# Moving TensorE's loop over extra expert blocks behind one matmul group, and the 64-token tile to the head of the last stage

## The chip, the cores and the metric

The kernel runs on one core of one Trainium2 chip. The metric is the device time of one execution in microseconds (us). Three runs of the kernel before gave 830.54, 830.91 and 832.59 us; the median is 830.91.

## What is computed

The reference is one step of a hybrid decoder layer over 512 prompt tokens and 64 sample tokens, 576 in all, with a model width of 1024. All of it is float32. Only its end matters here:

```python
    moe = jnp.zeros_like(h)
    for e in range(N_EXPERTS):
        gu = jnp.einsum('bld,df->blf', u, w_gate_up[e])
        hid = jax.nn.silu(gu[..., :D_EXPERT]) * gu[..., D_EXPERT:]
        moe = moe + combine[..., e:e + 1] * jnp.einsum('blf,fd->bld', hid, w_down[e])
    h = h + moe
    u = rmsnorm(h, norm_ple)
    gate = jax.nn.sigmoid(jnp.einsum('bld,de->ble', u, w_ple_gate))
    h = h + gate * jnp.einsum('blp,pd->bld', p_l, w_ple_proj)
    ...
    y = rmsnorm(h, norm_final)
```

Each token uses two of sixteen experts. The "input product" is `p_l @ w_ple_proj`, with 256 input channels; the "gate product" is `u @ w_ple_gate`, with 1024.

## The kernel before, in words

The 576 tokens are five tiles: tiles 0 to 3 of 128 tokens and tile 4 of 64. Every engine has one program in order, and semaphores tie the programs together.

**The expert stage.** Tokens are sorted into slots. Twelve phases of 128 slots (`NPH`) run through TensorE, which computes gate and up (L1348), transposes (L1361) and multiplies by the down weights (L1296). The results go to `y_slots` in HBM. Tokens that don't fit go into extra blocks of 32 slots. Extra block 0 is always computed, between the last phases (L1307, L1316, L1324, L1331). Further blocks are a loop that runs `n_ov - 1` times: TensorE reads `n_ov` from memory into a register (L1367), tests it (L1368) and loops (L1369). ScalarE, VectorE, GpSimd and SyncE have the same test in their own programs. In the trace the body of the loop runs on no engine: there is one extra block.

**The input products.** `p_product(t)` (L1376 to L1387) multiplies tile t's input by `w_proj`: 8 matmuls of 512 columns for a tile of 128 tokens, 16 of 256 for tile 4, whose columns go to two halves of the array (`sides`). Tile 0's product is made much earlier. `p_product(1)` waits until all results of the expert stage are out of PSUM (`y_ready` at 24), `p_product(3)` until ScalarE has copied out tile 1's. ScalarE copies each product to memory (`p_evac`, L1440 in the trace, since a helper records it) and counts `pp`. Behind tile 3's copy it loads the table for square roots (L1746).

**The last stage** goes over the tiles in the order `LAST`; k is the place in that order. Its steps for one k:

- GpSimd gathers two rows of `y_slots` per token (L2717, two indirect DMAs, j = 0 and 1) into one of two buffers. For k of 2 and more it first waits for `h3` to reach k: that is, combine(k - 2) has freed the buffer.
- VectorE's combine(k) (L2438) adds both to the residual `h2`, and counts `h3`: twice for k = 0 (by column halves), once for each later k.
- TensorE's `u3_transpose(k)` (L1401) makes eight transposes; VectorE's `u3_evac(k)` (L2449) copies them out in two halves with the gain, and counts `u3T`.
- ScalarE sums squares (L1751) and takes a root (L1754), for all five tiles before anything later; VectorE takes the reciprocal (`r3`, L2455).
- TensorE's gate product (L1419) runs in two column halves, hf 0 and hf 1. Between them stands `u3_transpose(k + 1)`. For k of 1 and more it begins when both halves of `u3_evac(k)` are done; for k = 0 the first half is enough to begin. For k of 2 and more each half waits for ScalarE's sigmoid of k - 2 as well.
- ScalarE takes the sigmoid (L1765) and squares (L1771) by halves, and a root (L1775); VectorE multiplies and adds (`gated`, L2462 and L2463), and `finish(k)` (L2481, L2486) scales the output row; SyncE stores it (L763, L765, L767) and loads the final gain (L758) when `h3` reaches 2.

VectorE's order is written out by hand, with k for the tile in that place:

```python
combine(0); u3_evac(0); combine(1); r3(0); combine(2); r3(1)
combine(3); u3_evac(1); r3(2); combine(4); r3(3); r3(4)
for k in range(NT):
    if 1 <= k < NT - 1: u3_evac(k + 1)
    for hf in range(2): gated(k, hf)      # and mean0 behind the first
    finish(k)
```

So `u3_evac(1)` stands behind combine(2) and combine(3), and `u3_evac(2)` behind all of `gated(0, ...)` and `finish(0)`. `LAST` is [0, 1, 4, 2, 3]: tile 4 is third.

Of the kernel before, what the change touches and what calls it, by code (L numbers as in the profile page):

```python
# [30 lines left out]
NT = 5  # L31
# [8 lines left out]
NOV = 32  # L40
# [4 lines left out]
RING = 3  # L45
GAMMA = [1.0 - 2.0 ** (-5.0 - h) for h in range(H)]
LEVELS = [2, 4, 8, 16, 32, 64]
LAST = [0, 1, 4, 2, 3]
HEADK = [(0, 1), (1, 2), (2, 4), (4, 6), (6, 8)]
ORDER = [4, 1, 0, 3, 2]  # L50
POS = {t: i for i, t in enumerate(ORDER)}
# [5 lines left out]
def ntok(t):  # L57
    return P if t < 4 else NB * LS


def sides(t):

    return [(slice(0, P), slice(0, 512))] if t < 4 else [(slice(0, 64), slice(0, 256)), (slice(64, P), slice(256, 512))]
# [283 lines left out]
def build(nc, a, o):  # L347
# [9 lines left out]
    with ExitStack() as ctx:  # L357
        def sb(name, shape, dt=F32):
            return ctx.enter_context(nc.sbuf_tensor(name, shape, dt))
# [3 lines left out]
        def sem(name):  # L363
            if name not in sems:
                sems[name] = ctx.enter_context(nc.semaphore(name))
            return sems[name]
# [4 lines left out]
        def C(name, n=P):  # L371
            off, w = CAT[name]
            return const[0:n, off:off + w]
# [177 lines left out]
        ovi = sb("ovi", [P, NOV + 1], U32)  # L551
# [124 lines left out]
        def _(sp):  # L676
# [82 lines left out]

            for k, t in enumerate(LAST):  # L760
                sp.wait_ge(sem("y_out"), k + 1)
# [11 lines left out]
        def _(pe):  # L773
# [24 lines left out]
            for s in STEPS:  # L798
# [52 lines left out]
                elif k0 == "tmv":  # L851
                    t = s[1]
# [6 lines left out]
                elif k0 in ("rTq", "rTk"):  # L859
                    t, n = s[1], ntok(s[1])  # L860
# [7 lines left out]
                elif k0 == "rS":  # L868
                    t, n = s[1], ntok(s[1])
# [9 lines left out]
                elif k0 == "rO":  # L879
                    t, n = s[1], ntok(s[1])  # L880
# [42 lines left out]
                elif k0 == "rU":  # L923
                    t = s[1]
# [60 lines left out]
                elif k0 == "gG":  # L985
                    t, n = s[1], ntok(s[1])
# [14 lines left out]
                elif k0 == "gs":  # L1001
                    t, n = s[1], ntok(s[1])
# [5 lines left out]
                elif k0 in ("gK", "gQ"):  # L1008
                    t, n = s[1], ntok(s[1])
# [7 lines left out]
                elif k0 == "gA":  # L1017
                    t, n = s[1], ntok(s[1])
# [5 lines left out]
                elif k0 == "lY":  # L1024
                    _, v, t = s
# [16 lines left out]
                elif k0 in ("lX", "lT"):  # L1042
                    _, v, t = s
# [19 lines left out]
                elif k0 in ("gV", "gk"):  # L1063
                    t, n = s[1], ntok(s[1])
# [7 lines left out]
                elif k0 == "gW":  # L1072
                    t, n = s[1], ntok(s[1])
# [8 lines left out]
                elif k0 == "gU":  # L1082
                    t, n = s[1], ntok(s[1])
# [5 lines left out]
                elif k0 in ("sD", "sDs"):  # L1089
                    t = s[1] if k0 == "sD" else 4  # L1090
# [19 lines left out]
                elif k0 == "sO":  # L1110
                    t, n = s[1], ntok(s[1])
# [30 lines left out]
                elif k0 == "sU":  # L1142
                    t = s[1]
# [15 lines left out]
                elif k0 in ("wo", "wh", "wg"):  # L1159
                    t = s[1]  # L1160
# [42 lines left out]
                elif k0 in ("x2a", "x2b", "x2c"):  # L1203
                    t, n = s[1], ntok(s[1])
# [6 lines left out]
                elif k0 == "rt":  # L1211
                    t, n = s[1], ntok(s[1])
# [8 lines left out]
                elif k0 == "rtT":  # L1221
                    t, n = s[1], ntok(s[1])
                    ev_wait(pe, ("rt", t))
                    nc.tensor.matmul(single[plan.buf[s]][0:n, 0:20], rtp[POS[t] % 2][:, 0:n], C("pick32"), start=True, stop=True).then_inc(s_mm, 1)
                elif k0 == "rank":
                    t, n = s[1], ntok(s[1])
                    i = POS[t]
# [9 lines left out]
                elif k0 == "ids":  # L1237
                    t, n = s[1], ntok(s[1])
                    i = POS[t]
# [62 lines left out]
            def ov_xpose(i):  # L1302

                pe.wait_ge(sem("ov_xg"), 16 * i + 16)
                pe.sem_inc(sem("ov_turn"), 1)
                for k in range(KD):
                    last = nc.tensor.transpose(single[0][:, BS * k:BS * k + BS], xg_ov[:, k * P:(k + 1) * P], C("ident")[0:BS, 0:BS])  # L1307
                last.then_inc(sem("ov_pe"), 1)

            def ov_gu(i):  # L1310

                pe.wait_ge(sem("ov_dve"), 3 * i + 1)
                pe.wait_ge(sem("ov_w"), 32 * i + 32)
                for k in range(KD):
                    for g in range(4):
                        last = nc.tensor.matmul(single[1][BS * g:BS * g + BS, 0:P], xT_ov[:, k, :], w_gu[0][:, k, P * g:P * g + P],  # L1316
                                                start=(k == 0), stop=(k == KD - 1))
                last.then_inc(sem("ov_pe"), 1)

            def ov_hT(i):  # L1320

                pe.wait_ge(sem("ov_dve"), 3 * i + 2)
                pe.sem_inc(sem("ov_turn"), 1)
                nc.tensor.transpose(single[0][:, DE:DE + 64], hid_ov, C("ident")[0:64, 0:64]).then_inc(sem("ov_pe"), 1)  # L1324

            def ov_down(i):

                pe.wait_ge(sem("ov_dve"), 3 * i + 3)
                for k in range(2):
                    for g in range(4):  # L1330
                        last = nc.tensor.matmul(single[1][BS * g:BS * g + BS, DE:2 * DE], hT_ov[:, BS * k:BS * k + BS],  # L1331
                                                w_dn_ov[:, k, DE * g:DE * g + DE], start=(k == 0), stop=(k == 1))
                last.then_inc(sem("ov_pe"), 1)
# [30 lines left out]
            down(NPH - 1)  # L1364
            ov_down(0)

            n_ov = pe.value_load(ovi[0:1, NOV:NOV + 1], min_val=0, max_val=NOV)  # L1367
            with pe.If(n_ov > 1):  # L1368
                with pe.Fori(1, n_ov) as i:  # L1369
                    ov_xpose(i)  # L1370
                    ov_gu(i)
                    ov_hT(i)
                    ov_down(i)

            def p_product(t):

                n = ntok(t)
                if t == 1:
                    pe.wait_ge(sem("y_ready"), 2 * NPH)
                elif t > 2:  # L1380
                    pe.wait_ge(sem("pp"), t - 1)
                for hf in range(2):
                    for k in range(2):
                        for rows, cols in sides(t):
                            last = nc.tensor.matmul(pair[t % 2][rows, hf, cols], pT[:, k, t * P:t * P + n],  # L1385
                                                    w_proj[:, k, hf * 512 + cols.start:hf * 512 + cols.stop], start=(k == 0), stop=(k == 1))
                last.then_inc(sem("pp_mm"), 1)  # L1387

            for t in range(1, NT - 1):
                p_product(t)  # L1390

            def u3_transpose(k):
                t, n = LAST[k], ntok(LAST[k])
                pe.wait_ge(sem("h3"), k + 2 if k else 1)
                if k >= 2:
                    pe.wait_ge(sem("u3T"), 2 * k - 2)
                for c in range(KD):
                    if k == 0 and c == 4:
                        pe.wait_ge(sem("h3"), 2)
                    out = single[2 * (k % 2) + c // 4][:, (c % 4) * n:(c % 4 + 1) * n]  # L1400
                    last = nc.tensor.transpose(out, h2[0:n, t, c * P:(c + 1) * P], C("ident")[0:n, 0:n])  # L1401
                last.then_inc(sem("u3_mm"), 1)

            p_product(NT - 1)
            u3_transpose(0)
            for k, t in enumerate(LAST):
                n = ntok(t)
# [19 lines left out]
        def _(act):  # L1427
# [13 lines left out]
            for s in STEPS:  # L1441
                k0 = s[0]
                if k0 == "ss":
                    for k in range(KD):
                        act.wait_ge(sem(f"ld_x{[k < hi for _, hi in HEADK].index(True)}"), 16)
                        nc.scalar.activation(xsq[:, k, :], uT[:, k, :], ACT.Square).then_inc(sem("xsq"), 1)
# [156 lines left out]
                elif k0 == "gA":  # L1603
# [7 lines left out]
                    last.then_inc(ev(k0), 1)  # L1611
                elif k0 == "lY":
                    _, v, t = s
                    n = ntok(t)
                    mm_wait(act, s)
# [120 lines left out]
            def p_evac(t):  # L1736

                act.wait_ge(sem("pp_mm"), t)
                for rows, cols in sides(t):
                    last = copy(pp[t][0:ntok(t)].rearrange("p (a b) -> p a b", a=2)[:, :, cols], pair[t % 2][rows, :, cols])  # L1740
                last.then_inc(sem("pp"), 1)
# [5 lines left out]
            p_evac(NT - 1)  # L1747
            for k, t in enumerate(LAST):
                n = ntok(t)
# [5 lines left out]
                                     scale=1.0 / D).then_inc(sem("ms_root"), 1)  # L1755
            for k, t in enumerate(LAST):
                n = ntok(t)
# [24 lines left out]
        def _(dve):  # L1782
# [650 lines left out]
            def combine(k):  # L2433
                t, n = LAST[k], ntok(LAST[k])
                for j in range(2):
                    dve.wait_ge(sem(f"ga{j}{k % 2}"), 16 * (k // 2 + 1))
                    for cols in ([slice(0, 512), slice(512, D)] if j and k == 0 else [slice(0, D)]):
                        ins = V.scalar_tensor_tensor(out=h2[0:n, t, cols], in0=ga[k % 2][j][0:n, cols], scalar=wcomb[0:n, j, POS[t]:POS[t] + 1],  # L2438
                                                     in1=h2[0:n, t, cols], op0=ALU.mult, op1=ALU.add)
                        if j == 0:  # L2440
                            link(ins)
                        else:
                            ins.then_inc(sem("h3"), 1)
# [346 lines left out]
```

## Time and profile before

| what | value |
|---|---|
| runs | 830.54, 830.91, 832.59 us |
| profiled execution, its own time | 833.75 us |
| its span | 831.9 us |
| mean granted clock of TensorE | 0.996 of full speed |
| PE (matmul) busy | 811.9 us, 98% |
| VectorE, ScalarE, GpSimd busy | 385.5, 213.8, 150.4 us |
| last matmul of the expert stage ends | 739.6 us after the span's start |
| last matmul of the kernel ends | 824.8 us |

The times in the profile count from the span's start. The chain that ended last is read back from the last instruction: each line of it is a start, a length, and an engine with its output and source line; "issue" is time in which the engine waited for nothing that the profile shows. Register loads, branches and DMA-issuing instructions are not counted as busy. A timeline merges like instructions; in brackets stands the idle time before them and what ended it.

### The profile page before, as it was taken

How to read it: one execution, taken by the hardware profiler on the slowest of the kernel's cores; microseconds unless marked ns; L12 is line 12 of the kernel's file. 1: busy time of each engine (PE TensorE's matmuls, PEld its weight loads, DVE VectorE, ACT ScalarE, POOL GpSimd, SP SyncE). 2: the span in 40 equal slices, each digit the busy share in tenths (PEclk: the TensorE clock that was granted, in tenths of full speed). 3: DMA queues.
4: the chain of work that ended last, by engine and by line, in shares of the span. 5: the costliest groups of instructions: out<-in, count | busy, mean ns of one | idle time of the engine just before them, and what ended most of it. 6: DMA issues, size and time to landing. Idle time of an engine off the chain costs nothing.

```text
span 831.9 us, 12853 instructions
## 1 busy us (share of the span) xinstructions
PE 811.9 (98%) x5194; PEld 509.7 (61%) x5194; DVE 385.5 (46%) x861; ACT 213.8 (26%) x462; POOL 150.4 (18%) x182
## 2 busy tenths in 40 slices
PE   9999999999999999999999999999999999989996
PEld 4545777887889987777777776455343333334452
DVE  3223457584666523664852559636441111005543
ACT  3211152339324311131001101022121111124554
POOL 0234321004055224200220053000100001004000
PEclk9999999999999999999999999999999999999999
DMA  9420354403020200522252024036899999976111
GB/s 363 201 101 10 119 184 152 141 32 110 1 102 3 92 12 13 202 89 84 101 202 100 2 102 180 21 110 253 328 355 406 424 423 410 416 292 222 51 39 51
DMA packets 20896, 135.23 MB, mean 163 GB/s; under 512 B 2420, under 2 KB 3060, under 8 KB 13668
## 3 DMA queue, kind: packets, MB, share of 16 engines
q1 hardware_dynamic: 13392, 103.34, 31.8%
q0 software_dynamic: 4720, 23.83, 7.8%
q10 hardware_dynamic: 2724, 7.21, 2.6%
q8 instruction: 43, 0.70, 0.3%
q14 instruction: 17, 0.14, 0.0%
HBM read 118.94 MB, written 19.63 MB: 167 GB/s over the span
## 4 chain that ended last, share of the span: by engine, by line
PE 46%; DVE 2%; issue 1%; ACT 1%; DVEq 0%; ACTq 0%
PE single L1348 10%; PE pair L1419 8%; PE pair L1200 6%; PE single L961 6%; PE pair L1296 5%; PE pair L982 2%; PE pair L1385 2%; PE single L982 2%; PE single L1281 1%; PE single L1256 1%; PE single L1361 1%; PE single L1401 1%; PE single L1209 0%; PE pair L1252 0%; DVE mem L2179 0%
## 5 line engine op out<-in xcount | busy, mean ns | idle before, releaser
L791 PE MATMUL pair<-mem 128*128 128x288 f32 x640 | 158.9, 408 | 0.0
L791 PEld LDWEIGHTS pair<-mem 128*128 128x128 f32 x640 | 120.3, 190 | 35.6 <-ACT mem L1440 2.1
L961 PE MATMUL single<-mem 128*128 128x288 f32 x448 | 110.0, 407 | 0.2
L961 PEld LDWEIGHTS single<-mem 128*128 128x128 f32 x448 | 84.7, 190 | 25.7 <-issue 1.6
L1348 PE MATMUL single<-mem 128*32 128x512 f32 x768 | 85.1, 594 | 0.9 <-DVE mem L2388 0.9
L1440 ACT ACTIVATE mem<-single 128x256 f32<-128x256 f32 (+5 forms) x109 | 44.6, 419 | 127.0 <-PE single L1209 48.5
L1440 ACT ACTIVATE mem<-pair 128x512 f32<-128x512 f32 (+5 forms) x77 | 33.0, 479 | 165.9 <-PE pair L791 63.1
L1419 PE MATMUL pair<-mem 128*128 128x512 f32 (+1 forms) x192 | 63.3, 524 | 0.8 <-DVE mem L2449 0.8
L1348 PEld LDWEIGHTS single<-mem 128*32 128x32 f32 x768 | 23.6, 110 | 52.8 <-issue 51.7
L2381 DVE SCALAR_TENSOR_TENSOR mem<-single,mem 128x256 f32<-128x256 f32 x12 | 5.8, 484 | 102.3 <-PE single L1348 91.1
L1200 PE MATMUL pair<-mem 128*128 128x512 f32 x112 | 51.0, 601 | 0.0
L1419 PEld LDWEIGHTS pair<-mem 128*128 128x128 f32 (+1 forms) x192 | 28.3, 172 | 32.6 <-issue 29.1
L1296 PE MATMUL pair<-mem 128*32 128x512 f32 x384 | 43.9, 595 | 0.0
L2100 DVE TENSOR_TENSOR mem<-mem,single 128x288 f32<-128x288 f32 x40 | 18.1, 452 | 55.7 <-PE single L961 52.2
L1200 PEld LDWEIGHTS pair<-mem 128*128 128x128 f32 x112 | 20.3, 190 | 21.7 <-issue 21.4
L856 PE MATMUL pair<-mem 128*128 128x512 f32 (+1 forms) x96 | 32.1, 525 | 0.0
L2687 POOL DMA_INDIRECT mem<-u_rows,ids x12 | 11.4, 948 | 110.6 <-PE single L1281 101.0
L832 PE MATMUL pair<-mem 128*128 128x512 f32 x64 | 28.2, 595 | 0.5 <-DVE mem L1812 0.5
L982 PE MATMUL pair<-mem 128*128 128x288 f32 x112 | 28.4, 409 | 0.2
L1898 DVE SCALAR_TENSOR_TENSOR mem<-mem,vec 128x512 f32<-128x512 f32 x36 | 27.9, 774 | 1.3
L982 PE MATMUL single<-mem 128*128 128x288 f32 x112 | 27.8, 406 | 0.0
L982 PEld LDWEIGHTS pair<-mem 128*128 128x128 f32 x112 | 21.0, 190 | 6.9 <-DVE mem L2152 1.3
(413 smaller groups left out, 1087.5 us busy)
## 6 DMA issues: line engine op xcount, KB each, us to landing
mem<-in_w_gu SPq DMA_DIRECT2D x17, 2048.0 KB, 14.7
mem<-in_w_down SPq DMA_DIRECT2D x17, 1024.0 KB, 13.8
y_slots<-mem SPq DMA_DIRECT2D x9, 512.0 KB, 11.0
y_slots<-in_zeros POOLq DMA_DIRECT2D x8, 512.0 KB, 8.0
mem<-in_w_ga SPq DMA_DIRECT2D x2, 2048.0 KB, 8.4
mem<-in_w_gb SPq DMA_DIRECT2D x2, 2048.0 KB, 7.8
mem<-in_w_wo SPq DMA_DIRECT2D x2, 2048.0 KB, 7.6
mem<-in_w_pg SPq DMA_DIRECT2D x2, 2048.0 KB, 17.3
```

Of the source, the lines that this page charges most:

```text
L791: last = nc.tensor.matmul(pb[:, hf, 0:HALF], w(k), rhs[:, k, hf * HALF:(hf + 1) * HALF], start=(k == 0), stop=(k == kk - 1))
L832: last = nc.tensor.matmul(q_bank[t][rows, cols], uT[:, k, t * P:t * P + ntok(t)], ring[0][:, 512 * k + cols.start:512 * k + cols.stop], st ...
L856: last = nc.tensor.matmul(pair[plan.buf[s]][rows, 0, cols], uT[:, k, t * P:t * P + ntok(t)], w[:, k, cols], start=(k == 0), stop=(k == KD ...
L961: last = nc.tensor.matmul(single[plan.buf[s]][:, 0:HALF], lhs[:, k, :], rhs[:, k, :], start=(k == 0 and j in (0, 1, 3, 4)), stop=(k == 3), ...
L982: last = nc.tensor.matmul(fast_bank(s), lhs[:, k, :], rhs[:, k, :], start=(k == 0 and j in (0, 1, 3, 4)), stop=(k == 1), skip_group_check= ...
L1200: last = nc.tensor.matmul(sx_bank[j], rows[:, u, v, :], wgt[:, u, 512 * v:512 * v + 512], start=(i == 0 and j < 5), stop=(i == 3), skip_gr ...
L1296: last = nc.tensor.matmul(pair[p % 2][BS * g:BS * g + BS, n, :], hT[p % 2][:, k, BS * g:BS * g + BS], w_dn[e % 4][:, k, n * 512:(n + 1) * ...
L1348: last = nc.tensor.matmul(single[3][BS * g:BS * g + BS, :], xT[p % 2][:, k, BS * g:BS * g + BS], w_gu[e % 4][:, k, :], start=(k == 0), sto ...
L1419: last = nc.tensor.matmul(pair[(k + 1) % 2][rows, hf, cols], u3T[:, c, t * P:t * P + n], w_pg[hf][:, c, cols], start=(c == 0), stop=(c == ...
L1440: copy = lambda out, in_, scale=1.0: nc.scalar.activation(out, in_, ACT.Copy, scale=scale)
L1898: V.scalar_tensor_tensor(out=acc[m % 2][:, 0:LP], in0=cbuf[m % 2][:, j:j + LP], scalar=conv_w[:, m, j:j + 1], in1=acc[m % 2][:, 0:LP], op0 ...
L2100: V.tensor_tensor(to, plus, single[plan.buf[s]][:, 0:HALF], ALU.add).then_inc(ev(k0), 1)
```

## The change

Two edits. TensorE's register load, test and loop move from before the input products to behind that of tile 1, so that its order is p_product(1), test, p_product(2), p_product(3), p_product(4). And `LAST` begins with the 64-token tile, on every engine that goes by it. The loops of the other engines stay where they are.

```diff
-LAST = [0, 1, 4, 2, 3]
+LAST = [4, 0, 1, 2, 3]
...
             ov_down(0)
 
-            n_ov = pe.value_load(ovi[0:1, NOV:NOV + 1], min_val=0, max_val=NOV)
-            with pe.If(n_ov > 1):
-                with pe.Fori(1, n_ov) as i:
-                    ov_xpose(i)
-                    ov_gu(i)
-                    ov_hT(i)
-                    ov_down(i)
-
             def p_product(t):
...
-            for t in range(1, NT - 1):
+            p_product(1)
+            n_ov = pe.value_load(ovi[0:1, NOV:NOV + 1], min_val=0, max_val=NOV)
+            with pe.If(n_ov > 1):
+                with pe.Fori(1, n_ov) as i:
+                    ov_xpose(i)
+                    ov_gu(i)
+                    ov_hT(i)
+                    ov_down(i)
+
+            for t in range(2, NT - 1):
                 p_product(t)
```

## Rows read from the trace of the kernel before

**Rows 1.** The page, part 1: busy time, share of span, instructions per engine.

```profile
PE 811.9 (98%) x5194; PEld 509.7 (61%) x5194; DVE 385.5 (46%) x861; ACT 213.8 (26%) x462; POOL 150.4 (18%) x182
```

**Rows 2.** The chain that ended last, 738 to 757: start, us, engine, line, count.

```profile
738.76 0.86 PE single L1331 x16
739.62 2.97 issue
742.59 14.14 PE pair L1385 x40
756.74 1.04 PE single L1401 x8
```

**Rows 3.** The same chain over the gate products.

```profile
766.55 13.74 PE pair L1419 x32
...
780.93 10.67 PE pair L1419 x48
...
803.28 0.87 PE single L1401 x8
804.16 20.62 PE pair L1419 x48
```

**Rows 4.** Busy time by stretch: length, engines' busy time, granted clock, DMA share.

```profile
742.60:756.74 14.14, 14.14 (x41) 6.20 (x42) 2.70 (x3) 3.87 (x4) 5.48 (x6) 0.88 0.56 189
```

**Rows 5.** The chain around a semaphore instruction of TensorE's own (L1305).

```profile
721.55 7.00 PE single L1348 x64
728.55 0.61 PE single L1307 x8
```

**Rows 6.** Timeline of VectorE: start, us, line, operation, count, idle before.

```profile
738.83 0.69 DVE L2425 COPY mem<-pair 128x512 f32<-128x512 f32 x1 [1.66 <-PE pair L1296]
750.77 1.28 DVE L2438 SCALAR_TENSOR_TENSOR mem<-mem,wcomb 128x1024 f32<-128x1024 f32 x1 [11.25 <-DMA mem<-y_slots,posu]
753.03 1.41 DVE L2438 SCALAR_TENSOR_TENSOR mem<-mem,wcomb 128x512 f32<-128x512 f32 x2 [0.98 <-DMA mem<-y_slots,posu]
...
759.00 2.59 DVE L2438 SCALAR_TENSOR_TENSOR mem<-mem,wcomb 128x1024 f32<-128x1024 f32 x2
```

**Rows 7.** Timeline of GpSimd: the gathers of the last stage.

```profile
746.54 0.95 POOL L2717 DMA_INDIRECT mem<-y_slots,posu  x1 [49.61 <-DMA y_slots<-mem]
747.79 0.94 POOL L2717 DMA_INDIRECT mem<-y_slots,posu  x1 [0.30 <-issue]
...
754.72 0.91 POOL L2717 DMA_INDIRECT mem<-y_slots,posu  x1 [3.50 <-DVE mem L2438]
...
761.87 1.80 POOL L2717 DMA_INDIRECT mem<-y_slots,posu  x1 [5.04 <-DVE mem L2438]
763.97 1.00 POOL L2717 DMA_INDIRECT mem<-y_slots,posu  x1 [0.30 <-issue]
```

**Rows 8.** Timeline of VectorE, from combine(3) to the second and third copies.

```profile
766.92 1.28 DVE L2438 SCALAR_TENSOR_TENSOR mem<-mem,wcomb 128x1024 f32<-128x1024 f32 x1 [2.69 <-DMA mem<-y_slots,posu]
769.18 1.28 DVE L2438 SCALAR_TENSOR_TENSOR mem<-mem,wcomb 128x1024 f32<-128x1024 f32 x1 [0.97 <-DMA mem<-y_slots,posu]
770.38 1.28 DVE L2449 TENSOR_TENSOR mem<-single,vec 128x512 f32<-128x512 f32 x2
...
771.65 2.58 DVE L2438 SCALAR_TENSOR_TENSOR mem<-mem,wcomb 128x1024 f32<-128x1024 f32 x2
...
785.83 0.75 DVE L2449 TENSOR_TENSOR mem<-single,vec 128x256 f32<-128x256 f32 x2
```

**Rows 9.** Timelines of ScalarE and VectorE: first sigmoids, and tile 4's round.

```profile
777.05 0.69 ACT L1765 ACTIVATE mem<-pair,ms 128x512 f32<-128x512 f32 x1
...
794.36 0.95 ACT L1765 ACTIVATE mem<-pair,ms 64x256 f32<-64x256 f32 x2
...
795.68 0.67 DVE L2462 TENSOR_TENSOR mem<-mem 64x512 f32<-64x512 f32 x1
...
804.20 1.29 DVE L2449 TENSOR_TENSOR mem<-single,vec 128x512 f32<-128x512 f32 x2
```

## The prediction

> **What bounds the kernel now.** I read the page's busy times first. TensorE's matmuls fill 98% of the span [rows 1], so time is saved only where TensorE idles or runs slowly, and lost wherever it is made to wait. The chain that ended last shows the first place. Behind the last matmul of the expert stage (738.76 + 0.86 = 739.62) stand 2.97 us of "issue", in which TensorE waits for nothing the profile shows [rows 2]. That is the register load and the test of the loop over extra blocks. Then come the four input products in 14.14 us. At full rate a matmul of 512 columns takes 13.74 / 32 = 0.43 us, and tile 4's 32 column-split ones take 10.67 - 16 x 0.43 = 3.8 us [rows 3]. So the four should take 3 x 8 x 0.43 + 1.9 = 12.2 us. The granted clock of that stretch was 0.88, a mixture of the levels 2.4 and 1.2 GHz [rows 4]: the idle gap cost 2.97 us, and the lower level behind it some 1.95.
>
> The timelines of GpSimd and VectorE show the second place. The last stage is fed by a relay of gathers. The first issues at 746.54, when the last stores of the expert stage have landed [rows 7], and the combined rows stand at 753.03 + 1.41 = 754.44 [rows 6]. TensorE is done with the input products only at 756.74, so at that moment it is TensorE that is late, by 2.3 us. A little later the relay is close behind: the copy `u3_evac(1)` ends at 771.66 [rows 8], and TensorE needs it when tile 0's gate product is half through the second 13.74, at 766.55 + 6.87 = 773.4 [rows 3]. `u3_evac(2)` ends at 786.6 [rows 8] and is needed at 780.93 + 6.87 = 787.8 [rows 3]. These two slacks, 1.8 and 1.2 us, are what the change plays with.
>
> **Part one, the test behind tile 1's product.** Nothing is added or removed; 16 instructions of TensorE (8 weight loads, 8 matmuls) move ahead of the load and the test. The product waits for the copies out of PSUM, which end at 739.52 [rows 6], so it starts at 739.6, at full clock, and ends at 743.05. The test runs beside it if TensorE's sequencer goes on while matmuls are queued. For that speaks a semaphore increment that TensorE's program has ahead of L1307: the matmuls on both sides of it join without a gap (721.55 + 7.00 = 728.55) [rows 5]. A register load from memory isn't such an increment, so both ends stay: wholly hidden, tile 2's product starts at 743.05; not hidden, at 746.0, with the lower clock again. I take 743.9: the 16 instructions issued in under 1 us, then the same gap, of which 0.9 us shows. Tiles 2, 3 and 4 then end at 743.9 + 2 x 3.43 + 1.9 = 752.7, which is 4.0 us earlier than now.
>
> The Trainium skill, "TensorE: Matmul & The Clock Gate", section "Part 2: What happens when you issue a matmul", says that the sequencer pops the next instruction as soon as it has committed one to the engine, and the table at its head gives TensorE's queue 64 places. By it the stage ends 4.0 us earlier; without it, at 756.7 as now. Against it stands "Runtime: NRT & Kernel Launch", section "Instruction fetch mechanics": a taken branch to a page that isn't loaded must wait for its fetch. No row here tells how much of the 2.97 us is such a fetch; as the fetch too would run beside queued matmuls, it would change the sum only if it came to more than the gap seen.
>
> Behind the waiting sequencer are tiles 2 to 4; ScalarE waits for tile 1's product, and gets it earlier.
>
> **Part two, tile 4 first.** No matmul is added. Tile 4's gate product takes 2 x 3.8 = 7.6 us where tile 0's takes 13.7, so TensorE asks for everything behind it 6 us sooner. The relay can't follow. VectorE's operations go by columns and cost the same for 64 rows as for 128. I follow the relay step by step.
>
> k = 0. Its gathers issue at 746.54 and 747.79 as now [rows 7]. They move half the bytes; the second lands at 753.03 now, and I take 752.3 (751.5 to 753.0: no row shows a landing of 64 rows by itself). combine(0) ends 1.41 later, 753.7; TensorE's transposes at 754.05, the copy (0.75 for 64 tokens, [rows 8]) at 754.8. TensorE starts the product behind the first half of the copy, 754.4, and without a wait would be through at 754.4 + 3.8 + 1.0 + 3.8 = 763.0, the 1.0 for the next tile's transposes [rows 2].
>
> k = 1. The gathers follow at once; the second issues at 750.3 and lands 5.24 later (747.79 to 753.03), at 755.5. combine(1) is two operations of 1.28 behind the copy: 757.2, against 759.00 + 2.59 = 761.6 now [rows 6]. So of the 4 us that TensorE gains, the relay takes 4.4 here.
>
> k = 2. Issued when combine(0) ends plus 0.28 [rows 6, 7]: 754.0 and 755.2. At 5.2 us each the second lands at 760.4; combine(2) ends at 761.7.
>
> k = 3. Issued 0.35 behind combine(1), 757.55; the second 1.25 to 2.1 later (between 761.87 and 763.97 it was 2.1, as the first took 1.80) [rows 7]. It lands 5.21 behind its issue (763.97 to 769.18): 764.4. combine(3) ends at 765.7, and `u3_evac(1)`, 1.28 long, at 767.0. Only then may TensorE begin k = 1: it **idles from 763.0 to 767.0**. That is the wait that takes the place of the one removed.
>
> k = 4. Issued behind combine(2), 762.0 and 763.25; landed at 768.5; combine(4) ends at 769.8. From there ScalarE's first sigmoid follows after 777.05 - (771.65 + 2.58) = 2.8 us: 772.6. Tile 4's round of sigmoid, `gated` and `finish` takes 804.20 - 794.36 = 9.84 us, less 0.37 in which VectorE was still busy with a copy (795.68 - 795.31) [rows 9]; for a tile of 128 it is 8.8. So `u3_evac(2)` ends at 772.6 + 9.5 + 1.29 = 783.4. TensorE would ask for it at 767.0 + 6.87 + 0.95 + 6.87 = 781.7, and at 783.65 if the 4.0 us of idle time bring the lower clock as the 2.97 did, at the same 1.95. I take the later, 783.7.
>
> From there all is TensorE's: 6.87 + 0.95 + 13.74 + 0.95 + 20.62 = 43.1 us (0.95 for eight transposes, between the 1.04 and 0.87 of [rows 2, 3]), end at 826.8. Now it ends at 804.16 + 20.62 = 824.8. The tail is the same, tile 3 being last in both. **Sum: +2.0 us**, against the profiled execution's own 833.75 us (span 831.9) 835.75. That execution is 2.84 above the median of the runs, and its last stage shows no reason for that; I put the 2.0 on the median: 832.9 us. The stores keep their places on SyncE's queue: every `y_out` comes in VectorE's order as before.
>
> The bounds of this case: with every gather landing 4.23 us behind its issue, as the first one does (746.54 to 750.77), `u3_evac(1)` ends at 764.2 and `u3_evac(2)` at 780.7, which is -1.0 us. With 1 us more in each of the three generations of gathers, as three loads at once could cost, it is +5.0.
>
> **Rivals.**
> - The test isn't hidden. Then `u3_transpose(0)` stays at 756.7, combine(1) ends at 760.8, `u3_evac(1)` at 771.1, combine(4) at 773.8, `u3_evac(2)` at 787.4, and the end comes at 830.5: +5.7 us, 836.6, slower. Its point: it decides once the input products end later than 753. For it: nothing in the trace shows TensorE's register load beside matmuls. Against it: the increment [rows 5].
> - The clock. TensorE idles 4 us before k = 1, longer than the 2.97 that brought the lower level. If that lasts twice as long as behind the first gap, TensorE asks at 785.6, +3.9 us, 834.8.
> - TensorE alone sets the time: the relay keeps up, and the 4.0 us of part one arrive whole, 826.9. For that `u3_evac(1)` must end by 763.0 and `u3_evac(2)` by 777.7, so combine(4) by 764.1, about when I expect the gather before it to land. Rows 7 and 8 speak against it.
> - The two parts cancel, within 1 us of zero: landings near the short bound.
>
> **How the numbers follow.** A measurement can tell about 0.3%, 2.5 us, from no change. My forecast's case has 0.64, of which 0.44 lies under +2.5 and 0.20 above; the test not hidden 0.16; the longer spell of low clock 0.10; cancelling 0.05; TensorE alone 0.05. So faster 0.05, within 0.3% 0.49, slower 0.46. The range runs from 830.0, near the short bound, to 836.7, which takes in the first rival; outside lie TensorE alone and the long end, together some 0.12.
>
> **What would show it.** Right: no issue gap between the expert stage and L1385, a gap of about 1 us behind its first 8 matmuls, a granted clock near 1.0 there; the input products over at about 752.7; TensorE idle some 4 us before the gate product of tile 0, released by VectorE's L2449; `u3_evac(2)` at about 783; the last matmul at 826.8. Wrong: the 2.97 us found whole behind tile 1's product (first rival), or TensorE without an idle gap at 763 (third), for which the gathers would have to land within 4 us.

## The result and the profile after

The changed kernel takes 836.72 us (median of 22 runs, 834.88 to 839.01). The kernel before, in 22 runs, now has a median of 833.31 us (830.39 to 835.54). The ratio is 1.0046 with an interval of 1.0036 to 1.0055: **the change costs about 0.46%, 3.8 us (3.0 to 4.6)**; the two medians alone differ by 3.4. The forecast was +2.0 us and 832.9 us, just inside the 0.3% that counts as no change, with a range up to 836.7. The loss lies beyond the 0.3%, and the median 0.02 us above the range. Two things put the time there. The median of three runs on which the 2.0 us were put, 830.91, is 2.4 us below the median of 22. And the sum itself is 1.3 us short, as the traces show: from the end of the expert stage to the end of the last gate product it was 824.78 - 739.62 = 85.2 us; now it is 828.06 - 739.52 = 88.5. The rest of this document calls that stretch **the stage**, and compares kernels by it, since it leaves out what happens before.

Executions of one kernel differ in TensorE's clock. In 78 runs of the kernel before, 31 have a mean granted clock of 0.997 or more and a median of 831.6 us; 47 have 0.996 or less and a median of 833.8. In the 14 profiles of this document, those without a lower clock in the stage show 0.997 or 0.998, those with one 0.993 to 0.996. The profiled executions of the kernel before (0.996) and of the changed kernel (0.993) have it.

TensorE's timeline of the changed kernel (start, us, line, operation, count; in brackets the idle time before and what ended it; lines left out are marked with dots). L1377, L1402 and L1420 are the lines that were L1385, L1401 and L1419:

```profile
738.47 1.05 PE L1331 MATMUL single<-mem 128*32 128x256 f32 x16
739.47 12.45 PE L1377 MATMUL pair<-mem 128*128 128x512 f32 x40
752.71 0.46 PE L1402 MATMUL single<-const,mem 64*128 64x64 f32 x4 [0.80 <-DVE mem L2439]
...
754.35 3.67 PE L1420 MATMUL pair<-mem 128*64 128x256 f32 x32 [0.52 <-DVE mem L2450]
757.95 1.09 PE L1402 MATMUL single<-const,mem 128*128 128x128 f32 x8
758.98 3.67 PE L1420 MATMUL pair<-mem 128*64 128x256 f32 x32
767.77 9.57 PE L1420 MATMUL pair<-mem 128*128 128x512 f32 x16 [5.12 <-DVE mem L2450]
...
778.06 13.90 PE L1420 MATMUL pair<-mem 128*128 128x512 f32 x32
```

The first wait is gone: all 40 matmuls of the four input products join the expert stage without a gap, at 12.45 us where [rows 2] has 2.97 + 14.14. The second wait has taken its place, 5.12 us before tile 0's gate product, and behind it 16 matmuls take 9.57 us. In the windows of the changed kernel (stretch, busy time of PE, PEld, DVE, ACT and POOL, then the granted clock of TensorE) the clock falls in that wait and comes back late:

```profile
764.00:768.00 4.00, 0.23 (x1) 0.23 (x2) 3.94 (x6) 1.41 (x3) 0.21 (x1) 0.74 0.69 248
768.00:772.00 4.00, 4.00 (x5) 1.62 (x6) 2.49 (x4) 1.66 (x5) 0.00 (x0) 0.50 0.01 2
772.00:776.00 4.00, 4.00 (x10) 1.77 (x9) 1.37 (x2) 2.51 (x4) 0.00 (x0) 0.91 0.00 0
776.00:780.00 4.00, 4.00 (x17) 2.25 (x16) 1.51 (x3) 2.48 (x7) 0.00 (x0) 1.00 0.00 0
```

0.50 is the level of 1.2 GHz: in 4 us that TensorE is wholly busy it does 5 matmuls, where 13.74 / 32 us for one [rows 3] would make 9. VectorE's timeline of the changed kernel says why TensorE waits (`combine` is L2439, the copy `u3_evac` L2450):

```profile
759.14 2.62 DVE L2439 SCALAR_TENSOR_TENSOR mem<-mem,wcomb 128x1024 f32<-128x1024 f32 x2 [1.94 <-DMA mem<-y_slots,posu]
...
763.90 2.62 DVE L2439 SCALAR_TENSOR_TENSOR mem<-mem,wcomb 128x1024 f32<-128x1024 f32 x2 [2.06 <-DMA mem<-y_slots,posu]
766.44 1.28 DVE L2450 TENSOR_TENSOR mem<-single,vec 128x512 f32<-128x512 f32 x2
...
782.53 1.27 DVE L2450 TENSOR_TENSOR mem<-single,vec 128x512 f32<-128x512 f32 x2
```

`u3_evac(1)` needs combine(1), which was over at 757.1, and TensorE's transposes of it, over at 759.04. But it stands behind combine(2) and combine(3), and combine(3) waits 2.06 us for its gather. The chain of the changed kernel runs through that gather, which took 6.47 us from its issue to its landing, and then through TensorE alone to the end:

```profile
757.40 6.47 DMA mem<-y_slots,posu
...
766.52 1.21 DVE mem L2450 x2
...
767.77 9.57 PE pair L1420 x16
...
778.22 13.73 PE pair L1420 x32
...
807.44 20.62 PE pair L1420 x48
```

The second copy, `u3_evac(2)`, ends at 782.53 + 1.27 = 783.80. TensorE gets to it only at 778.06 + 7.03 = 785.1, so there it doesn't wait.

### The profile page after: what moved, and what is told of

Its sections match the earlier page's. It is cut to its first block, busy times and chain, and to the rows that moved or that the text cites. A ratio compares the mean times of both kernels' runs of the same rounds, so it can differ in the third digit from the quotient of the medians.

```text
span 835.2 us, 12853 instructions
## 1 busy us (share of the span) xinstructions
PE 812.3 (97%) x5194; PEld 510.3 (61%) x5194; DVE 385.7 (46%) x861; ACT 214.0 (26%) x462; POOL 150.4 (18%) x182
## 4 chain that ended last, share of the span: by engine, by line
PE 43%; DVE 3%; DMA 2%; issue 1%; ACT 1%; POOL 0%; DVEq 0%; POOLq 0%; ACTq 0%
PE single L1348 10%; PE pair L1420 7%; PE pair L1200 6%; PE single L961 6%; PE pair L1296 5%; PE pair L982 2%; PE single L982 2%; PE single L1281 1%; DMA mem<-y_slots,posu 1%; DVE mem L2439 1%; DMA y_slots<-mem 1%; PE single L1256 1%; PE single L1361 1%; PE single L1209 0%; PE pair L1252 0%
## 5 line engine op out<-in xcount | busy, mean ns | idle before, releaser
L1420 PE MATMUL pair<-mem 128*128 128x512 f32 (+1 forms) x192 | 65.5, 537 | 5.6 <-DVE mem L2450 5.6
L1420 PEld LDWEIGHTS pair<-mem 128*128 128x128 f32 (+1 forms) x192 | 29.4, 177 | 38.6 <-issue 30.4
L856 PE MATMUL pair<-mem 128*128 128x512 f32 (+1 forms) x96 | 32.1, 525 | 0.0
```

What stands on the lines that cost most here:

```text
L856: last = nc.tensor.matmul(pair[plan.buf[s]][rows, 0, cols], uT[:, k, t * P:t * P + ntok(t)], w[:, k, cols], start=(k == 0), stop=(k == KD ...
L1420: last = nc.tensor.matmul(pair[(k + 1) % 2][rows, hf, cols], u3T[:, c, t * P:t * P + n], w_pg[hf][:, c, cols], start=(c == 0), stop=(c == ...
```

## The experiments

The theory: the order of tiles is the loss, by the order of VectorE's copies; the move of the test is a small gain by itself. The rivals: the move of the test does harm, the lower clock is the whole loss, or the gathers are too slow for any order.

### One part at a time

Only the test moved (the changed kernel with the old `LAST`):

```diff
-LAST = [4, 0, 1, 2, 3]
+LAST = [0, 1, 4, 2, 3]
```

> Only the first part: the test behind tile 1's product, LAST as before (tile 0 first, tile 4 third). Theory (the first part gains, the second gives it back): the input products end at about 751.9 as in the changed kernel, but the first gathered tile of 128 rows is combined at 754.4, so TensorE's gate product of tile 0 starts at about 755.5 instead of 758.5. Tile 0's product of 13.7 us and its transposes last until 770.2, u3_evac(1) ends at about 769.4, so no wait; u3_evac(2) at 784.4 against 784.6, so hardly one. End 3 us earlier than before: -2.5 to -3.1 us, 0.3 to 0.4% faster. Rival (the first part itself is what costs, for instance because an earlier start drags the gathers or copies): slower than before or within 1 us of it.

Measured: 831.76 us, ratio 0.9980 (0.9969 to 0.9990), a gain of 1.7 us; the stage takes 84.0 us, 1.2 less than before. TensorE's timeline:

```profile
742.11 12.45 PE L1377 MATMUL pair<-mem 128*128 128x512 f32 x40
756.41 1.32 PE L1402 MATMUL single<-const,mem 128*128 128x128 f32 x8 [1.86 <-DVE mem L2439]
758.51 8.55 PE L1420 MATMUL pair<-mem 128*128 128x512 f32 x16 [0.79 <-DVE mem L2450]
```

The gap is gone, as with both parts. But TensorE now is ahead of the gathers: it waits 1.86 us for combine(0) and 0.79 for the copy, and in this execution the lower clock comes behind these waits instead, 8.55 us for 16 matmuls that take 7.13 at full clock. This execution, with 835.13 us and a mean clock of 0.996, is the longest of the twelve; nine of them show 0.997 or more. The gain is real and smaller than I put it.

Only the tile moved (the kernel before with the new `LAST`, the test in its old place):

> Only the second part: tile 4 first, the test at its old place ahead of all input products. Theory: the input products end at 756.7 as before, combine(1) at 760.8, u3_evac(1) at 771.1, and TensorE idles 4.6 us before the second tile, with the lower clock behind it, which costs 2.7 us as in the changed kernel; end at 830.5 to 831.5, +5.7 to +6.7 us, 0.7 to 0.8% slower. Rival (the order of tiles is harmless, the loss comes from the moved test): within 1 us of before.

Measured: 839.57 us, ratio 1.0056 (1.0035 to 1.0077), 4.7 us lost; stage 89.6. TensorE's timeline:

```profile
742.24 12.45 PE L1385 MATMUL pair<-mem 128*128 128x512 f32 x40 [0.91 <-issue]
...
769.00 9.60 PE L1419 MATMUL pair<-mem 128*128 128x512 f32 x16 [4.59 <-DVE mem L2449]
...
787.71 7.13 PE L1419 MATMUL pair<-mem 128*128 128x512 f32 x16 [1.36 <-DVE mem L2449]
```

The whole loss is in this part: the wait for `u3_evac(1)` with the lower clock behind it, and here also 1.36 us for `u3_evac(2)`. Together with the 1.7 us that the other part gains it is 3.0, the low end of the interval of what both lose. By the stages of one execution each, the parts make -1.2 and +4.4, together 3.2, and both at once 3.3. The nine runs fall into two groups, five at 839.57 to 840.75 us and four at 835.00 to 836.63; the profiled one, 839.91, is of the upper group. The gap of the test was only 0.91 us in this execution; more on that below.

### How much of it is the lower clock

The wait kept, but TensorE kept busy in it, by five matmuls on constants whose output nobody reads (each is two in the trace):

```diff
                     if hf == 0 and k + 1 < NT:
                         u3_transpose(k + 1)
+                    if hf == 1 and k == 0:
+                        for _ in range(5):
+                            nc.tensor.matmul(single[0][:, :], C("ones"), const[:, 0:512], ...)
```

> The changed kernel, with five matmuls of 512 columns on constants added behind the first tile's gate product; they write to a PSUM bank that nobody reads, 4.3 us of work in the 5.1 us in which TensorE waits for u3_evac(1). Nothing of the relay of gathers changes. Theory (1.3 us of the loss is the lower clock behind the wait): the product of tile 0 takes 6.9 us for its first half instead of 9.6, TensorE then waits for u3_evac(2) at 783.8, and the kernel ends 1.3 us earlier than the changed one, at about +2.0 us against before. Rival (the wait alone sets the loss and the clock is hidden behind u3_evac(2)): the same time as the changed kernel, +3.4.

Measured: 835.97 us, ratio 1.0030 (1.0019 to 1.0042), some 1.3 us less loss by the ratios, whose intervals just overlap. Its profiled execution, one of 840.04 us, isn't typical: ten of the twelve lie between 834.83 and 836.59. In it gathers came late, TensorE waited 3.63 us for `u3_evac(2)`, and the stage took 91.0. So here is a second profile of it, beside a second one of the changed kernel:

> The changed kernel with the five matmuls on constants again, for a second look at what its first profiled execution left unclear: there the gap was filled and the clock kept, but the fifth gather landed 2.3 us later than in the changed kernel and the wait before the third tile took the gain back (91.0 us from the end of the expert stage). Theory (the clock is worth about 1.3 us, the late gather was a draw of its own): about 87.2 us, with a wait of at most 1.5 us before the third tile. Rival (filling the gap delays the gathers): again 3 us or more of wait there, 90 to 92 us.

> The changed kernel, unchanged, for a second profiled execution. From the end of the expert stage to the end of the last matmul it took 88.5 us in the first, with 5.1 us of wait before tile 0's product and 2.7 us of lower clock behind it. Theory (the relay of gathers and VectorE's order set the waits): the same wait within 1.5 us, the lower clock again, 88 to 90 us in all. Rival (the first execution was a chance draw): a wait under 3 us and a stage of under 86.5 us.

Measured: filled 836.25 us and a stage of 87.8; changed 837.25 us and 88.6. TensorE's timeline of the filled one:

```profile
762.55 4.56 PE L1427 MATMUL single<-const 128*128 128x512 f32 x10
767.49 7.13 PE L1420 MATMUL pair<-mem 128*128 128x512 f32 x16 [0.38 <-DVE mem L2453]
...
784.02 7.13 PE L1420 MATMUL pair<-mem 128*128 128x512 f32 x16 [1.66 <-DVE mem L2453]
```

and of the changed one:

```profile
767.76 9.78 PE L1420 MATMUL pair<-mem 128*128 128x512 f32 x16 [4.87 <-DVE mem L2450]
```

The wait and its low clock come again in the second profile of the changed kernel (4.87 us, then 9.78). With the wait filled the same 16 matmuls take 7.13 us, 2.65 less, but only 0.8 of that reaches the end: TensorE then waits 1.66 us for `u3_evac(2)`. The lower clock is part of the loss, and VectorE's relay, about 1 us behind it, is the next bound.

### Where VectorE's order holds it

`u3_evac(1)` ahead of combine(3) in VectorE's order, all else as changed:

```diff
-            combine(3)
             u3_evac(1)
+            combine(3)
```

> The changed kernel with one line moved: in VectorE's order u3_evac(1) stands ahead of combine(3) instead of behind it. Theory (two stations of the relay stand close behind each other): the wait of 5.1 us before tile 0's product shrinks to about 0.4 us, but TensorE then asks for u3_evac(2) at 777.7 while VectorE does it at 783.1, still behind gated(0) and finish(0). So a wait of 5.4 us comes one tile later, with the lower clock behind it: between +1.3 us (no clock cost) and +4.0 us against before, no gain on the changed kernel. Rival (only the copy's place behind combine(3) holds TensorE back): about -4 us against before, 0.5% faster.

Measured: 839.27 us, ratio 1.0067 (1.0052 to 1.0081); stage 91.3. It is worse than the changed kernel. TensorE's timeline:

```profile
763.81 7.13 PE L1420 MATMUL pair<-mem 128*128 128x512 f32 x16 [1.33 <-DVE mem L2450]
...
785.02 9.65 PE L1420 MATMUL pair<-mem 128*128 128x512 f32 x16 [6.33 <-DVE mem L2450]
```

The first wait shrinks from 5.12 to 1.33 us, and TensorE runs through it at full clock. But `u3_evac(2)`, behind all of tile 4's round, comes no earlier, so the wait moves one tile on, becomes 6.33 us, and has the lower clock behind it (9.65). The second copy moved alone was not run; in the changed kernel it is ready before TensorE asks for it, so by that trace it has nothing to give without the first. Both moved:

```diff
-            combine(3)
             u3_evac(1)
+            combine(3)
...
             r3(4)
+            u3_evac(2)
             for k in range(NT):
-                if 1 <= k < NT - 1:
+                if 2 <= k < NT - 1:
                     u3_evac(k + 1)
```

> The changed kernel with both copies early in VectorE's order: u3_evac(1) ahead of combine(3), and u3_evac(2) ahead of the first gated instead of behind finish(0). Theory (the order of VectorE's program, not the gathers, holds TensorE back): the wait before the second tile is about 1.3 us as in the run with only the first copy early, the wait before the third is gone since the copy can end at about 774.5 and is asked for at 778.5, and no lower clock comes behind it. The last matmul ends some 3 us earlier than in the profile of before, which is 2 to 4 us below before's median, 0.2 to 0.5% faster. Rival (the gathers themselves are too late for a 64-token tile at the head, whatever VectorE's order): TensorE waits elsewhere, and the time stays within 1.5 us of the changed kernel, +2.5 or more.

Measured: **830.01 us, ratio 0.9967 (0.9953 to 0.9982), 2.8 us faster than before**; stage 81.1, which is 7.4 us less than the changed kernel's and 4.1 less than before. TensorE's timeline:

```profile
753.78 3.67 PE L1420 MATMUL pair<-mem 128*64 128x256 f32 x32 [0.52 <-DVE mem L2450]
...
758.41 10.94 PE L1420 MATMUL pair<-mem 128*64 128x256 f32 x48
...
770.06 13.90 PE L1420 MATMUL pair<-mem 128*128 128x512 f32 x32
```

and VectorE's:

```profile
760.89 1.27 DVE L2450 TENSOR_TENSOR mem<-single,vec 128x512 f32<-128x512 f32 x2
...
771.56 1.27 DVE L2450 TENSOR_TENSOR mem<-single,vec 128x512 f32<-128x512 f32 x2
```

The second half of tile 4's product and the first of tile 0's are one run of 48 matmuls: no wait is left there, and none before tile 1. The copies end at 762.2 and 772.8 instead of 767.7 and 783.8. Gathers no faster at the end were enough: combine(4) is over at 769.9 here, and at 770.3 in the changed kernel. So it was the order of VectorE's queue that kept TensorE waiting. That the first wait is wholly gone is in part this execution's gathers: combine(2) was over at 760.9, in the run with only the first copy moved at 762.5, and with the same order up to there that run waited 1.33 us.

### Are the early copies good by themselves

The copies early, with the test moved but the tiles in the old order:

> LAST as before, the test behind tile 1's product, and both copies early. Theory: with tile 0 first the copies were in time already in the run of the first part alone, so moving them is worth nothing: the same as that run, -1.7 us against before within 0.8. Rival (the early copies give something of their own): 1.5 us or more below that run.

Measured: 837.07 us, ratio 1.0055 (1.0035 to 1.0075); stage 87.4. That is a miss: it loses what the changed kernel loses. VectorE's timeline:

```profile
781.85 0.76 DVE L2450 TENSOR_TENSOR mem<-single,vec 128x256 f32<-128x256 f32 x2 [6.29 <-PE single L1402]
782.52 0.68 DVE L2463 TENSOR_TENSOR mem<-mem 128x512 f32<-128x512 f32 x1
```

and TensorE's:

```profile
800.43 7.13 PE L1420 MATMUL pair<-mem 128*128 128x512 f32 x16 [3.33 <-DVE mem L2450]
```

In the old order TensorE reaches the transposes for `u3_evac(2)` 10 us later than with tile 4 first (781.10 - 741.66 = 39.4 us into the stage, against 769.18 - 739.56 = 29.6). VectorE, whose order is fixed, stands 6.29 us in front of that copy, and `gated(0, ...)`, which could have run, queues behind it. Everything of VectorE is later from there, and TensorE pays at the fourth tile. These 3.33 us have no lower clock behind them: the 16 matmuls take 7.13. So the copies belong early only with tile 4 first: the order of tiles and VectorE's order are one decision.

The tile first and both copies early, with the test in its old place:

> Tile 4 first and both copies early, but the test at its old place. It prices the first part in a last stage that can use it. Theory (the input products' end sets the start of this stage): with a gap of 0.9 us in front of them, as in one execution with the test there, the kernel is 0.8 us slower than the run with all three edits (-3.6 against before); with a gap of 2.9 us and the lower clock, as in the two executions of the kernel before, 4.5 us slower. So between -2.8 and +0.9 us against before. Rival (the gathers set the start, the first part is worth nothing here): -3.6 us against before, the same as with all three edits.

Measured: 832.45 us, ratio 0.9994 (0.9977 to 1.0010); stage 81.7, with a gap of 0.90 us at the test. Against the run with all three edits (0.9967, stage 81.1) the move of the test is worth 0.3% by the ratios, whose intervals just overlap, and 0.6 us by the stages of one execution each.

### What the test is worth

The kernel before, with TensorE's load, test and loop over further extra blocks left out:

> The kernel before without TensorE's register load, test and loop (nothing else is changed; the loop's body runs on no engine in this data). It prices the test. Theory (behind tile 1's product the test is wholly hidden): the same time as the run of the first part alone, -1.7 us within 0.8. Rival (part of the test still costs there): 1.5 us or more below that run.

Measured: 832.58 us, ratio 0.9992 (0.9977 to 1.0007), no difference that these runs can show; stage 85.8. TensorE's timeline:

```profile
754.53 1.47 PE L1393 MATMUL single<-const,mem 128*128 128x128 f32 x8 [2.12 <-DVE mem L2430]
756.79 9.90 PE L1411 MATMUL pair<-mem 128*128 128x512 f32 x16 [0.78 <-DVE mem L2441]
```

Without any test TensorE is 2.12 us too early for combine(0), and in this execution, whose mean clock of 0.995 is the lowest of the twelve, the lower clock moves there whole: 9.90 us for 16 matmuls. So in the old order the 2.97 us of [rows 2] were worth little, between these 0.7 us, which aren't clear of zero, and the 1.7 of the test moved: the wait goes over to the gathers.

The same, filled: the test moved, the old `LAST`, and two matmuls on constants (four in the trace) between the last input product and the first transposes:

```diff
             p_product(NT - 1)
+            for _ in range(2):
+                nc.tensor.matmul(single[2][:, :], C("ones"), const[:, 0:512], ...)
             u3_transpose(0)
```

> The run of the first part alone (test moved, LAST as before) with two matmuls of 512 columns on constants behind the input products, 1.7 us of work in the 1.9 us in which TensorE waits for the first combined tile; they write to a PSUM bank that nobody reads then. Theory (the wait brings the lower clock, which takes back 1.4 to 1.7 us of the first part's gain): the first half of tile 0's gate product takes 7.1 us for its 16 matmuls instead of 8.6, and the kernel comes to -2.8 to -3.1 us against before instead of -1.7. Rival (the clock's loss is hidden by a later wait): the same as the first part alone, -1.7 us.

Measured: 831.97 us, ratio 0.9989 (0.9976 to 1.0002); stage 82.4, 1.6 less than with the test moved alone. TensorE's timeline:

```profile
754.35 1.98 PE L1407 MATMUL single<-const 128*128 128x512 f32 x4
...
758.15 7.13 PE L1422 MATMUL pair<-mem 128*128 128x512 f32 x16 [0.78 <-DVE mem L2452]
```

The lower clock is gone (7.13 for 8.55) and the stage is shorter by about that, but the median isn't: it was a miss. The granted clocks point to the reason: all twelve runs here show 0.997 or more, but so did nine of the twelve without the fill, whose median is 831.4 us. Most of those had no lower clock to win back; the profiled one had. No profile of one of the nine shows it directly.

The kernel before, profiled once more for its gap:

> The kernel before, unchanged, for a second profiled execution of it. The first showed 2.97 us between the expert stage and the input products and 1.95 us of lower clock behind it; the run with only the second part showed 0.91 us at the same place and full clock. If the gap is a fixed cost it is 2.97 here too; if it differs between executions, it lies anywhere between 0.9 and 3.0, and where it is short the input products end at about 752.7 after the same start.

Measured: 833.8 us, stage 85.4. TensorE's timeline:

```profile
742.38 14.14 PE L1385 MATMUL pair<-mem 128*128 128x512 f32 x40 [2.93 <-issue]
```

The gap and the lower clock behind it come again. But this execution too has a mean clock of 0.996, as 47 of the 78 runs at most have. The other 31, at 0.997 or more, should by the profiles' clocks have no lower clock in the stage; none of them was profiled, so how long their gap is stays open.

## Why the prediction was wrong, and what of it was right

The path was right: the first wait goes, a wait for `u3_evac(1)` takes its place, and the loss is small. From the forecast 832.9 us to the measured 836.72 it is 3.8 us. Of these 2.4 are the base, and 1.4 the sum (1.3 by the traces).

**Part one.** I took 0.9 us of the test as visible; none was. The input products ended at 751.9 instead of 752.7. The first rival, a test that isn't hidden, is out. The Trainium skill, "TensorE: Matmul & The Clock Gate", section "Part 2: What happens when you issue a matmul", has the sequencer take the next instruction as soon as one is committed; the trace agrees, with 0 us of gap where 2.97 stood. The 0.8 us were worth nothing, because the gathers set combine(0).

**The relay.** It came nearly as worked out: combine(0) at 753.3 (taken 753.7), combine(1) at 757.1 (757.2), combine(2) at 761.8 (761.7), `u3_evac(2)` at 783.8 (783.4). One term of it was mis-sized: combine(3) ended at 766.5 and not 765.7. I let the second of its two gathers set it, 5.21 us behind its issue; in fact the first landed only 6.47 us behind its own, at 763.87, and both operations came behind that. In the second profile the second gather took 6.24 us, and combine(3) ended at 766.5 again. `u3_evac(1)` was 0.7 us late by it, and the wait 5.12 instead of 4.0 (TensorE also got there at 762.65, not 763.0).

**The sum, where a step failed: TensorE's ask for `u3_evac(2)`.** I had TensorE ask at 783.65 and the copy ready at 783.4, and let the sum end there. Measured, the copy was ready at 783.8, but TensorE asked at 785.1. Past that point every further 0.1 us of TensorE's goes to the end. Two terms made it late, by about as much each. One is the gather just named. The other is the price of the lower clock, which I took from the gap before, at 1.95 us: from its start at 767.77 TensorE needed 17.3 us to the ask, where I had 16.6. Like for like, 14.14 - 12.45 = 1.7 us behind the gap of 2.97 became 9.57 - 7.13 = 2.4 us behind the wait of 5.12. With both terms the ask was 1.3 us later than the copy.

**The second rival** put the bound there too, TensorE's own clock. It was priced at +3.9 us, with 785.6 for the ask; measured is 785.1, +3.3 in the traces and +3.8 by the ratio. That it comes so near is in part luck: its condition was a clock price of twice 1.95 us, and that was 2.4; the late gather made up the rest. I gave it 0.10, as the trace had shown the price of a shorter wait only.

**The base, the other step that failed.** I knew that the profiled execution, 833.75 us, stood 2.84 above the median of three and saw no reason in its last stage; I put the sum on the median. With 22 runs the median is 833.31, so the profiled execution was the better base: 833.75 + 3.3 = 837.05, and the profiled execution of the changed kernel took 837.02. The runs point to a reason in the last stage after all, the lower clock behind the gap. All three runs lie below 833.26 us, the shortest of the 47 with a mean clock of 0.996 or less. So by the profiles' clocks they were of the kind without a lower clock in the stage, and the sum counted as a gain what they didn't lose. That rests on times and mean clocks; no such execution was profiled.

**The third rival**, TensorE alone, needed combine(4) by 764.1. It was right that the relay can't do that in this order, but the condition was too narrow: it took VectorE's order as given. With the two copies moved, TensorE's stage is 4.1 us shorter than before, with combine(4) at 769.9.

**The short bound** of the range gave `u3_evac(1)` at 764.2. By its own steps I get about 764.8; as `u3_evac(2)`, at 780.7, sets that case, its -1.0 us stay.

**The order of the argument.** I named VectorE's written order in the prediction's own steps, combine(3) ahead of `u3_evac(1)` and tile 4's round ahead of `u3_evac(2)`, and that is the cause that the runs confirm: moving only the first copy moves the wait, moving both takes it away.

## What to carry to other kernels

When one engine is made earlier, follow it to the next station of the relay, and read the queue order of the engine that feeds it: a shorter tile in front pays only when the copies for the tile behind it are moved up in the same edit (-0.33% instead of +0.46% here). An idle spell of TensorE can be priced twice, once as the wait and once as a lower clock behind it, and shortening one wait can move both to the next. Where two bounds come within a few tenths of a us of each other, give both a fair chance, and put a sum made from a trace on that trace's own time or on a ratio, not on a median of three runs: the mean granted clock tells whether the runs and the profiled execution are of one kind.

## What the runs showed of the hardware

**The gap of a register load and a test isn't a constant.** At the same place in TensorE's program it was 2.97 and 2.93 us in the kernel before, and 0.91 and 0.90 with the other order of tiles. With 16 instructions of matmul work put ahead of it, it was 0 in all nine profiles. What makes the long one long is open; the two short ones are also the two with the longer start that is told below.

**The length of a wait doesn't tell its price in clock.** Two waits of 2.12 and 0.78 us were followed by 9.90 us for 16 matmuls (7.13 at full clock), 1.86 and 0.79 by 8.55, 3.63 by 8.83, 4.59 by 9.60, 6.33 by 9.65; waits of 1.33, 1.36 and 1.66 us cost nothing, and neither did the one of 3.33 in the run with the test moved and both copies early, through which the granted clock stayed at 1.00.

**GpSimd's gather takes twice as long to issue beside a combine.** GpSimd's timeline of the changed kernel:

```profile
753.59 0.93 POOL L2718 DMA_INDIRECT mem<-y_slots,posu  x1 [2.77 <-DVE mem L2439]
754.82 1.80 POOL L2718 DMA_INDIRECT mem<-y_slots,posu  x1 [0.30 <-issue]
```

The second began 0.28 us into combine(1), which starts at 754.54 and reads two operands from the on-chip memory SBUF. The 1.80 of [rows 7] stands in the same place, 0.28 us behind a combine's start. The Trainium skill, "SBUF — State Buffer", section "SBUF: two separate sides", says that a VectorE operation with two inputs from SBUF and a GpSimd operation that reads SBUF share a pair of ports, which the first to start holds for its whole instruction; 1.80 against 0.93 agrees with that. Two experiments show it with and without the combine. The first gather of the last tile, with only the test moved, began 0.23 us into a combine:

```profile
766.29 1.87 POOL L2718 DMA_INDIRECT mem<-y_slots,posu  x1 [2.27 <-DVE mem L2439]
```

With both copies early as well, VectorE stood idle at that moment:

```profile
765.84 0.94 POOL L2719 DMA_INDIRECT mem<-y_slots,posu  x1 [2.38 <-DVE mem L2439]
```

**The start of the kernel isn't the same in all profiles.** The first large group of matmuls, from 5.68, took 20.87 us in the kernel before, and 23.06 in the run with only the test moved. In the windows over that line the difference is in the first matmuls, kernel before:

```profile
8.00:11.00 3.00, 3.00 (x9) 1.33 (x8) 1.00 1.03 414
```

and the test moved:

```profile
8.00:11.00 3.00, 3.00 (x6) 1.20 (x5) 1.00 1.03 415
```

Six matmuls instead of nine, with 1.00 as granted clock in both. Five of the experiments' profiles had this longer start, 22.66 to 23.30 us; they are the five kernels that have exactly one of the change's two edits. The kernel before, the changed kernel and the rest, with second profiles of three of them, had 20.87. So it may belong to the program, but no kernel with it was profiled twice. If it does, the ratios of those five kernels hold some 2 us that aren't the last stage's. That is why stages are compared here.
